# Six up units of each SwiGLU layer as seven half-size products in an fp32 block stack on one Trainium2 core

## What is computed

```
D_MODEL, SEQ = 1024, 512
D_FF = ((8 * D_MODEL // 3 + 255) // 256) * 256      # 2816
def swiglu(h, w_gate, w_up, w_down):
    return (jax.nn.silu(h @ w_gate) * (h @ w_up)) @ w_down
...
        h = rms_norm(x, ffn_norm[i])
        x = x + swiglu(h, ffn_w_gate[i], ffn_w_up[i], ffn_w_down[i])
```

## Time and profile before

| | us |
|---|---|
| median of 3 runs (2022.41 to 2023.0) | 2022.54 |
| the profiled execution | 2022.42 |
| its span, first to last instruction | 2020.7 |

### The profile page before, as it was taken

How to read it: one execution, slowest core, us unless ns; L and a number is a source line. 1 busy time by engine, 2 the same in 40 slices (tenths; PEclk the granted TensorE clock), 3 DMA queues, 4 the chain that set the end, 5 groups by cost and what they waited for, 6 DMA issues and landing times.

```text
span 2020.7 us, 27320 instructions
## 1 busy us (share of the span) xinstructions
PE 2002.4 (99%) x10444; PEld 1669.3 (83%) x10444; DVE 979.5 (48%) x1486; ACT 941.8 (47%) x1607; POOL 1159.5 (57%) x937
## 2 busy tenths in 40 slices
PE   9999999999999999999999999999999999999998
PEld 7888899888877778898888788988897887777787
DVE  3184644542244336554632388777885234442321
ACT  4124443522244446334522387677675235554542
POOL 4445877675533215877765558878886442413342
PEclk9999999999999999999999999999999999999999
DMA  5233333233432212332333434343433331112131
GB/s 172 88 100 101 98 105 105 84 86 101 116 105 84 88 60 84 103 107 85 97 86 101 118 105 128 107 124 105 118 107 89 105 91 63 63 63 84 42 104 63
DMA packets 259569, 193.61 MB, mean 96 GB/s; under 512 B 9555, under 2 KB 247431, under 8 KB 259448
## 3 DMA queue, kind: packets, MB, share of 16 engines
q1 hardware_dynamic: 256188, 190.67, 31.5%
q10 hardware_dynamic: 3260, 1.28, 0.3%
HBM read 189.66 MB, written 2.27 MB: 95 GB/s over the span
## 4 chain that ended last, share of the span: by engine, by line
PE 57%; issue 23%; POOL 15%; ACT 2%; DVE 2%; DMA 1%; POOLq 0%; SPq 0%; ACTq 0%; DVEq 0%
POOL wlo L782 14%; PE bank L2494 12%; PE bank L2495 12%; PE bank L2496 12%; PE bank L2711 5%; PE bank L2712 5%; PE bank L2713 5%; PE bank L3071 1%; PE bank L3067 1%; PE bank L3035 1%; POOL f0aLo L818 1%; DVE xc L2077 1%; DMA rows<-cums 1%; POOL wlo L851 0%; DVE xC L2077 0%
## 5 line engine op out<-in xcount | busy, mean ns | idle before, releaser
L782 POOL TENSOR_TENSOR wlo<-raw,whi 128x512 fp32r<-128x512 f32 (+1 forms) x532 | 669.9, 1290 | 693.4 <-ACT whi L940 678.4
L940 ACT ACTIVATE whi<-raw 128x2048 fp32r<-128x2048 f32 (+1 forms) x131 | 233.0, 1779 | 310.6 <-PE bank L2496 301.8
L2494 PE MATMUL bank<-hHi,whi 128*128 128x512 f32 (+1 forms) x880 | 349.9, 398 | 2.3 <-POOL wlo L782 1.4
L2496 PE MATMUL bank<-hHi,wlo 128*128 128x512 f32 (+1 forms) x880 | 341.5, 388 | 0.0
L2495 PE MATMUL bank<-hLo,whi 128*128 128x512 f32 (+1 forms) x880 | 341.2, 388 | 0.0
L803 POOL TENSOR_TENSOR wlo<-raw,whi 128x512 fp32r<-128x512 f32 x144 | 193.2, 1365 | 81.3 <-ACT whi L1105 81.3
L2494 PE MATMUL bank<-whi,hHi 128*128 128x256 f32 (+1 forms) x640 | 219.3, 343 | 0.4 <-issue 0.3
L2496 PE MATMUL bank<-whi,hLo 128*128 128x256 f32 (+1 forms) x640 | 208.5, 326 | 0.0
L2495 PE MATMUL bank<-wlo,hHi 128*128 128x256 f32 (+1 forms) x640 | 208.3, 325 | 0.0
L2494 PEld LDWEIGHTS bank<-hHi,whi 128*128 128x128 f32 x880 | 165.4, 188 | 42.3 <-issue 5.1
L2496 PEld LDWEIGHTS bank<-hHi,wlo 128*128 128x128 f32 x880 | 165.2, 188 | 34.8
(11 more groups left out here) (458 smaller groups left out, 4143.9 us busy)
## 6 DMA issues: line engine op xcount, KB each, us to landing
raw<-in_ssd_w_in SPq DMA_DIRECT2D x48, 512.0 KB, 4.9
raw<-in_ffn_w_gate SPq DMA_DIRECT2D x44, 512.0 KB, 4.4
raw<-in_ffn_w_up SPq DMA_DIRECT2D x44, 512.0 KB, 4.6
raw<-in_gla_w_in SPq DMA_DIRECT2D x40, 512.0 KB, 4.6
rows<-cums SPq DMA_DIRECT2D x64, 256.0 KB, 5.6
raw<-in_ffn_w_down SPq DMA_DIRECT2D x32, 384.0 KB, 3.6
raw<-in_attn_w_qkv SPq DMA_DIRECT2D x24, 512.0 KB, 4.4
raw<-in_conv_w_in SPq DMA_DIRECT2D x23, 512.0 KB, 4.4
```

What stands on the lines that cost most here:

```text
L782: ins = pool.tensor_tensor(wlo[s][:, part], raw[s][:, part], whi[s][:, part].bitcast(F32), ALU.subtract)
L940: act.activation(whi[s][:, 0:w], raw[s][:, 0:w], ACT.Copy).then_inc(w_hi, 1)
L2494: pe.matmul(dst, hi1, hi2, start=first, stop=False)
L2496: return pe.matmul(dst, lo1, hi2, start=False, stop=last)
```

## The change

In pairs 3 to 8 (BOTH) the up unit is a product of seven quarters, too, called v11, vS2, vS1, vS3, v12, v22, vS4, each times 256 columns. The turns of such a pair are BOTH_TURNS, 14 in place of 11. Four sums are made on DVE (`first_up_sums`, `last_up_sums`; vS1 and vS4 in the tiles `t32`, vS3 and vS2 in place in `raw1`), three running sums in bank 4 are copied by ACT into `upkept`, four half blocks are added on DVE (`up_block`) into `plain`, and `up_product` multiplies `plain` by silu and by rstd. ORDER lists all 106 quarters of a layer. As 106 isn't a multiple of 8, SLOT_AT spreads six skipped ring slots over the layer; `turned_ahead` gives the count that ACT waits for. Some areas in SBUF move (`room`, `under`, `spare`).

```diff
+BOTH_TURNS = ["11", "12", "S2", "S1", "S3", "22", "v11", "S4", "vS2", "vS1", "vS3", "v12", "v22", "vS4"]
+BOTH = (3, 4, 5, 6, 7, 8)
...
+SKIPPED = -QUARTERS % 8
+SLOT_AT = []
+for _r in range(QUARTERS):
+    SLOT_AT.append(_r + min(SKIPPED, max(0, _r - 8) * (SKIPPED + 1) // (QUARTERS - 16)))
...
+def turned_ahead(r):
+    return len([at for at in SLOT_AT if at <= SLOT_AT[r] - 8])
...
# SP
+                    if s and i in BOTH:
+                        return [late("q_lo", turned_by(j, i, "v22")), late("s_made", 4 * summed_units(j, i, True) + 4)]
...
# ACT
+                def both_sevens(i):
+                    kept(i, 0, "11")
+                    kept(i, 1, "S2")
+                    turn_high(i, "vS2")
+                    turn_high(i, "vS1")
+                    kept(i, 2, "S3")
+                    for name in ("vS3", "v12", "v22"):
+                        turn_high(i, name)
+                    kept(i, 3, "v11")
+                    turn_high(i, "vS4")
+                    turn_high(i + 1, "11")
+                    kept(i, 4, "vS2")
+                    gate_silu(i, 0, 1)
+                    turn_high(i + 1, "12")
+                    gate_silu(i, 1, 0)
+                    kept(i, 5, "vS3")
+                    for name in turns(i + 1)[2:8]:
+                        turn_high(i + 1, name)
...
# DVE
+                def first_up_sums(i):
+                    n = u_up + 2 * i + 1
+                    dve.wait_ge(raw_full[1], 32 * (n // 2 + 1))
+                    if i > BOTH[0]:
+                        dve.wait_ge(*late("q_lo", turned_by(j, max(k for k in BOTH if k < i), "vS4")))
+                    tt(source(j, i, "vS1"), raw_quarter(1, 1, 0), raw_quarter(1, 1, 1), ALU.add).then_inc(L("s_made"), 1)
+                    tt(source(j, i, "vS3"), raw_quarter(1, 0, 0), raw_quarter(1, 1, 0), ALU.subtract).then_inc(L("s_made"), 1)
+                def last_up_sums(i):
...
+                    dve.wait_ge(*late("q_lo", turned_by(j, i, "v11")))
...
+                def up_block(i, b, half, kept, src, name):
...
+                    tt(to, kept_part(j, i, 3 + kept), src[:, 0:256], ALU.add).then_inc(L("c_made"), 1)
+                def up_product(i, b, blocks):
...
+                    chain(tt(plain(j, 2 * i + b), plain(j, 2 * i + b), tile(sil, b), ALU.mult))
+                    tt(plain(j, 2 * i + b), plain(j, 2 * i + b), rstd[:, :], ALU.mult).then_inc(S(f"a_done{j}"), 1)
...
+                def both_sevens(i):
+                    first_up_sums(i)
+                    block(i, 0, 0, 0, bank[2], "12")
+                    last_up_sums(i)
+                    block(i, 1, 1, 2, bank[1], "S1")
+                    block(i, 1, 0, 2, bank[3], "22")
+                    first_sums(i + 1)
+                    scaled(i, 1, 3)
+                    block(i, 0, 1, 1, bank[1], "S4")
+                    scaled(i, 0, 4)
+                    last_sums(i + 1)
+                    up_block(i, 1, 1, 2, bank[5], "vS1")
+                    up_block(i, 0, 0, 0, bank[6], "v12")
+                    up_block(i, 1, 0, 2, bank[7], "v22")
+                    up_product(i, 1, 3)
+                    up_block(i, 0, 1, 1, bank[5], "vS4")
+                    up_product(i, 0, 4)
...
# PE
+                def up_sevens(i, v):
+                    quarter(bank[4], i, "v11", half(0, 0), True, 256)
+                    pe.wait_ge(*late("c_made", 4 * v + 2))
+                    quarter(bank[1], i, "S4", half(1, 1), False, 256)
+                    pe.wait_ge(*late("kept", 3 * v + 4))
+                    quarter(bank[4], i, "vS2", summed(i, 2, 0), False, 256)
+                    pe.wait_ge(S(f"a_done{j}"), 2 * i + 1)
+                    quarter(bank[5], i, "vS1", summed(i, 0, 1), True, 256)
+                    pe.wait_ge(*late("kept", 3 * v + 5))
+                    quarter(bank[4], i, "vS3", summed(i, 1, 2), False, 256)
+                    quarter(bank[6], i, "v12", half(1, 0), True, 256)
+                    quarter(bank[7], i, "v22", summed(i, 3, 3), True, 256)
+                    pe.wait_ge(*late("c_made", 4 * v + 5))
+                    quarter(bank[5], i, "vS4", half(1, 1), False, 256)
```

More of the change, by code:

```diff
@@ L259, in build @@
         m_ffn = [area([(f"f{j}aHi", [P, FT * SEQ], F32R), (f"f{j}aLo", [P, FT * SEQ], F32R),
-                       (f"f{j}sil", [P, 2 * SEQ], F32)]) for j in range(2)]
+                       (f"f{j}room", [P, 3 * 256], F32), (f"f{j}sil", [P, 2 * SEQ], F32)]) for j in range(2)]
         m_seven = [area([(f"f{j}sums", [P, 16 * SEQ], F32R), (f"f{j}wsum", [P, 3 * SEQ], F32), (f"f{j}kept", [P, 3 * SEQ], F32),
-                         (f"f{j}plain", [P, FT * SEQ], F32)]) for j in range(2)]
+                         (f"f{j}plain", [P, FT * SEQ], F32), (f"f{j}upkept", [P, 3 * 256], F32)])
+                   for j in range(2)]
         att_spec = [("qk", [P, 2 * KT * SEQ], F32), ("vtok", R8, F32)]
@@ L326, in turned_by, with summed_units @@
             return QUARTERS * j + turn_at(i, name) + 1
-        def seven(j, i):
-            return SEVENS * j + i - FIRST_SEVEN
+        def summed_units(j, i, up=False):
+            return SUMMED * j + i - FIRST_SEVEN + len([k for k in BOTH if k < i]) + up
         def slot(buf, j, i, name):
-            q = turn_at(i, name) % 8
+            q = SLOT_AT[turn_at(i, name)] % 8
             return buf[q // 4][:, SEQ * (q % 4):SEQ * (q % 4 + 1)]
@@ L830, in ffn @@
                 for i in range(FIRST_SEVEN, LAST_SEVEN + 1):
-                    for name in TURNS:
+                    for name in turns(i):
                         turn_low(j, i, name)
@@ L1109, in kept @@
                     act.wait_ge(*late("q_mm", turned_by(j, i, name)))
-                    copy(kept_part(j, i, n), bank[0][:, 0:256], L("kept"))
+                    if n >= 3 and i > BOTH[0]:
+                        k = max(k for k in BOTH if k < i)
+                        act.wait_ge(*late("c_made", 4 * summed_units(j, k, True) + 4))
+                    copy(kept_part(j, i, n), bank[4 if n >= 3 else 0][:, 0:256], L("kept"))
+                def both_sevens(i):
[16 more added lines that the diff above has]
+                        turn_high(i + 1, name)
                 def sevens(i):
+                    if i in BOTH:
+                        both_sevens(i)
+                        return
                     kept(i, 0, "11")
@@ L1132, in sevens @@
                     gate_silu(i, 1, 0)
-                    for name in ("S2", "S1", "S3", "22", "u0", "S4"):
+                    for name in turns(i + 1)[2:8]:
                         turn_high(i + 1, name)
@@ L1173, in ffn @@
                 pair(1)
-                for name in TURNS[:8]:
+                for name in turns(FIRST_SEVEN)[:8]:
                     turn_high(FIRST_SEVEN, name)
@@ L1868, in first_sums @@
                     tt(source(j, i, "S3"), raw_quarter(0, 0, 0), raw_quarter(0, 1, 0), ALU.subtract).then_inc(L("s_made"), 1)
+                def first_up_sums(i):
[6 more added lines that the diff above has]
+                def last_up_sums(i):
+                    s0 = 4 * summed_units(j, i, True)
+                    dve.wait_ge(*late("s_made", s0 + 2))
+                    dve.wait_ge(*late("q_lo", turned_by(j, i, "v11")))
+                    tt(source(j, i, "vS2"), source(j, i, "vS1"), raw_quarter(1, 0, 0), ALU.subtract).then_inc(L("s_made"), 1)
+                    dve.wait_ge(*late("s_made", s0 + 3))
+                    tt(source(j, i, "vS4"), raw_quarter(1, 0, 1), source(j, i, "vS2"), ALU.subtract).then_inc(L("s_made"), 1)
+                def up_block(i, b, half, kept, src, name):
+                    dve.wait_ge(*late("kept", 3 * summed_units(j, i, True) + kept + 1))
+                    dve.wait_ge(*late("q_mm", turned_by(j, i, name)))
+                    to = plain(j, 2 * i + b)[:, 256 * half:256 * half + 256]
+                    tt(to, kept_part(j, i, 3 + kept), src[:, 0:256], ALU.add).then_inc(L("c_made"), 1)
+                def up_product(i, b, blocks):
+                    dve.wait_ge(*late("c_made", 4 * summed_units(j, i, True) + blocks))
+                    dve.wait_ge(S(f"sil_ready{j}"), 2 * i + (1 - b) + 1 + 1)
+                    chain(tt(plain(j, 2 * i + b), plain(j, 2 * i + b), tile(sil, b), ALU.mult))
+                    tt(plain(j, 2 * i + b), plain(j, 2 * i + b), rstd[:, :], ALU.mult).then_inc(S(f"a_done{j}"), 1)
                 def last_sums(i):
-                    s0 = 4 * seven(j, i)
+                    s0 = 4 * summed_units(j, i)
                     dve.wait_ge(*late("s_made", s0 + 2))
@@ L2740, in sevens @@
                     if again:
[L2741 removed]
+                        pe.wait_ge(*late("c_made", 4 * was + 4))
                     else:
@@ L2752, in sevens @@
                     quarter(bank[3], i, "22", summed(i, 3, 3), True, 256)
-                    if again:
+                    if i - 1 in BOTH:
+                        pe.wait_ge(*late("kept", 3 * v))
+                    elif again:
```

(3 more changed lines are left out.)

48 lines of the change are left out of this document (31 added, 17 removed).

## The result

| | us |
|---|---|
| kernel before, median of 4 runs (2022.36 to 2023.0) | 2022.47 |
| with the change, median of 4 runs (2068.89 to 2071.65) | 2069.72 |
| span of the profiled execution after | 2067.2 |

What follows compares the result with a forecast made beforehand. TensorE bounds the kernel before; with the change POOL's round would: 17.5 + 2.42 + 1.48 + 4.05 = 25.45 us a pair, +4.45. A layer costs 0.6 + 5 x 4.45 = 22.85, both +45.7: 2068, range 2046 to 2082.

Steps and rivals of the forecast that it cites:

- TensorE's own work falls: In a pair's up unit, four 512-column quarters (10.94 us) become seven of 256 (10.08): -0.86 us a unit, pair 20.14.
- 14 low halves at 1.25, nine delays of 0.45: POOL's round in a pair: 17.5 us of low halves, plus 4.05 us for nine DVE operations clashing at the SBUF port.
- wait A: POOL idles ahead of vS2, as DVE's vS3 gets the port only after S4's low half: 2.42 us a pair.
- wait B: POOL idles for the next pair's sum S2, which stands at the port until quarter 12's low half ends: 1.48 us.
- the one of 0.60: Rival: a DVE operation holds the port for its whole instruction, 0.60 us a delay; pair 26.8, total 2084; chance 0.06.
- Waits A and B: POOL's two waits for DVE's sums in its round, 2.42 and 1.48 us a pair.
- not a bound by time: DVE with four more sums and four half blocks is busy some 14.7 us of a pair's 20.14.
- Pair 3 and pair 9: Pair 3, cushioned by POOL's lead, idles once for 1.4 us and takes 21.6 (+0.6); in pair 9 TensorE runs through.
- the clock falls too: Rival: TensorE's clock falls in pauses, hidden in steady pairs but not the first: +3 us a layer, 2074; chance 0.13.
- TensorE stays the bound: Rival, faster: POOL keeps up in the six pairs, so TensorE's saving of 10.3 us shows, 2012; chance 0.05.
- the rival's condition: For TensorE to stay the bound: POOL meets at most five DVE operations a pair and waits for no sum.
- The skipped ring slots, the later load, the moved areas at nothing: ACT's extra ring wait (42 of 106 turns), SP's later up-weight load and moved SBUF areas were put at no cost.

Runs made afterwards that it cites:

- e6: e5 with the seven products in pairs 2, 4, 6 and 8 only, so rstd from PSUM and the early block; 2014.23 us, ratio 0.9959 to the kernel before.
- e3: The change with the four multiplications by rstd in a pair reading PSUM bank 7 instead of the SBUF copy, v22 moved to bank 6; 2039.58 us, ratio 1.0086.
- e1: The change with DVE's up block of vS1 put ahead of the next pair's sums S2 and S4; 2063.22 us, ratio 1.0203.
- e5: e3 and e1 together in the same six pairs: rstd from PSUM, block of vS1 ahead of the next pair's sums; 2036.1 us.
- e7: The change in three pairs only, BOTH = (3, 5, 7), rstd from SBUF and old order; 2032.48 us, ratio 1.0051.
- e9: e6 without the early block: block of vS1 behind the next pair's sums again; 2020.12 us, ratio 0.999.
- e8: The change with sum S2 in a tile of its own (acc), so it no longer waits for quarter 11's low half; 2057.75 us.

## Why the prediction was right

- *TensorE's own work falls*: right. 84 matmuls at 0.120 replace 48 at 0.2275. e6 shows it as time: its pairs of fourteen take 20.15 us in place of 21.00, and it is 8.3 us faster for 8 units (0.86 x 8 = 6.9, inside the interval of 5.5 to 10.9). Not all of the 8.3 is TensorE's work: over the whole span TensorE waited 2.0 us for POOL's low halves outside the sevens parts (L2494) before, and 0.6 in e6.
- *14 low halves at 1.25, nine delays of 0.45*: right, counted in the timeline. That the port and not the amount of work makes the delays is shown by e3. The nine are those that I named: vS3, vS2 and vS4 pass in wait A, S2 and S4 in wait B. The price from the rows, 0.45, held, and not the one of 0.60: by that the round would have been 17.5 + 9 x 0.60 + 3.64 = 26.5, it is 25.23. The trace agrees with the Trainium skill (SBUF — State Buffer, "Who interferes with whom") on who clashes, and on DVE's side also on how long: DVE stands until the low half has ended. The low half behind a DVE operation comes 0.45 late, less than DVE's pace of 0.60; no run shows which part of the operation holds the port.
- *Waits A and B*: right in place, 2.29 and 1.35 where I had 2.42 and 1.48. The 0.13 too much is in both: I took the hand-over as 1.48 from the start of a sum that ran at once (0.68 us to its end). A sum that has stood at the port ends sooner after the low half: 0.55 us for S2 (300.37 to 300.92). The steady pair is 25.23, forecast 25.45, which is 1.1 us a layer less. TensorE's pauses are up to 3.5 ahead of vS4 (forecast 3.7) and, in pair 4, 1.4 ahead of S4 (forecast 1.5), counted from start to start less one pace of 0.12.
- *DVE "not a bound by time"*: right in the end, wrong in size. It is busy for 21.67 us a pair and not 14.7; the 7 us are its stands at the port, which the sum of its durations left out.
- *Pair 3 and pair 9*: mis-sized. In layer 0 pair 3 starts at 256.41 and pair 4 at 278.33, so pair 3 takes 21.92 us, +0.92 where I had +0.6, as its pause is 1.7 and not 1.4. In pair 9 I had TensorE "run through" at no cost. Pair 10 starts at 427.21 in place of 403.41, 23.8 us later. The stretch ahead of pair 3 gives 0.16 of that (it started at 256.25 before), pair 3 gives 0.92, and the five rounds of 25.24 (276.79 to 403.00) give 21.2. That leaves 1.5 for the stretch behind the last pause, and there the clock is down:

```profile
403.00:407.00 4.00, 4.00 (x23) 4.00 (x24) 3.90 (x6) 2.33 (x5) 4.00 (x3) 0.67 0.02 4
```

From 404.3 to 407.8 some fifteen matmuls are 0.213 us apart in place of 0.120, which is 1.4. This is the rival "the clock falls too", true in part beside the forecast. The loss is hidden in the steady pairs, as I had said (length 25.23 at 1.00 and at 0.89), but it comes at the end, where no pause follows that could hide it, and not in the first pairs. In layer 1 it is absent: pair 9 takes 21.16 us there, as before, and the layer's sevens part is 22.2 us longer. So the rival's +3 a layer was 1.4 in one layer. The Trainium skill, TensorE: Matmul & The Clock Gate, Part 1, gives 1.2 GHz for an idle array and 2.4 GHz for a busy one; the trace agrees with these two levels, though here the lower one stands while TensorE works, after a pause.
- *The total*: partly luck. The steady pairs were forecast 2.1 us too long in all, and pair 3 and the clock at the end, with what lies outside the sevens, made up for it.
- *TensorE stays the bound*, the rival on the other side: wrong for six pairs in a row. In e6 TensorE is the bound (0.2 us of waits), but not under the rival's condition: POOL still waits twice 1.35 us for sums in a pair of fourteen and makes up its lead in the pair of eleven behind it.
- *The skipped ring slots, the later load, the moved areas at nothing*: not tried alone. In the sevens part of layer 0 no pause of TensorE ends on a DMA or on a low half, neither with the change nor in e6, and POOL's two waits in the round end on the high halves of sums. e6, which has the moved areas, the later load and four skipped slots, has 0.2 us of such pauses in all. So they cost TensorE nothing that these traces show.

## What to carry over

When work moves from the busiest engine to a second one, count for the second not its busy share but its round: its pieces, the delays at a shared port, and the waits for what it must be given, and see whether its idle time was what kept clashes free of charge. A pause stands where a delay comes to light, which need not be where it is made; moving the instruction that ends it wins little if another engine's round sets the pace (6.5 of 47 us in e1). Reading one operand from PSUM kept a VectorE operation off the port that GpSimd needs (in e3 the scaling took 0.67 us in place of 1.77, and the four such operations of a pair brought 30 us in all), and spacing the heavy steps let the ring of eight slots carry the lead (e6 against e5).

## What the runs showed beyond that

- The lower clock doesn't double the pace of these matmuls: 0.213 us apart at 1.2 GHz, 0.120 at 2.4 GHz with 256 columns (1.8 times).
- The clock does not fall in the pause alone. After the one that ended at 403.00 TensorE started at full pace, and fell about 1.3 us later, in PE's timeline:

```profile
404.18 0.29 PE L2821 MATMUL bank<-hHi,whi 128*128 128x256 f32 x1
404.30 0.38 PE L2822 MATMUL bank<-hLo,whi 128*128 128x256 f32 x1
404.48 0.42 PE L2823 MATMUL bank<-hHi,wlo 128*128 128x256 f32 x1
404.69 0.42 PE L2821 MATMUL bank<-hHi,whi 128*128 128x256 f32 x1
```
- Some kernels with such pauses spread more from run to run: 2.8 us for the change and 3.4 for e7 (four runs each), 3.9 for e9 (ten), against 0.7 for e6 (five) and 1.6 for the kernel before (thirteen). e1, e3, e5 and e8 had two runs each, which can't show it.
